# Experts in fixed places of 32-row grains, and a router that picks tile by tile

## What is computed

```python
def _hier_moe(h, w_r1, b_r1, w_r2, b_r2, w13, w2):
    p_grp = softmax(h @ w_r1 + b_r1); grp = argmax(p_grp)              # 4 groups
    p_in = softmax((einsum('nd,gde->nge', h, w_r2) + b_r2)[rows, grp]) # 8 experts in a group
    top_p, top_j = top_k(p_in, 2); top_p /= sum(top_p)
    expert = grp * 8 + top_j;  wts = p_grp[grp] * top_p                # 32 experts in all
    for each expert e, for its tokens:
        g, u = split(h[tok] @ w13[e]); y = (silu(g) * u) @ w2[e]       # 1024 -> 2 x 512 -> 1024
    out[tok] += wts * y
```

## Time and profile before

| | |
|---|---|
| median of 3 runs | 3217.28 us (3216.04 to 3217.42) |
| the profiled execution's own time | 3216.31 us |
| its span, first to last instruction | 3214.7 us |
| PE busy | 2896.9 us (90%) |
| DVE, ACT, POOL busy | 1299.6, 792.7, 689.5 us |
| expert loads L1616, L1857, L1859 | 216 of 2048 KB |
| L1707 (gate_up), L1728 (down) busy | 707.9, 352.8 us |

### The profile page before, as it was taken

The page is one execution under the profiler, slowest core; times in us unless marked ns, Lnnn a source line. Parts: engine busy times, 40 slices in busy tenths (PEclk is TensorE's granted clock), DMA queues, the critical chain, the costliest instruction groups (busy, mean ns, idle before and its releaser), DMA issues. The chain is left out here.

```text
span 3214.7 us, 34383 instructions
## 1 busy us (share of the span) xinstructions
PE 2896.9 (90%) x13041; PEld 1615.1 (50%) x13041; DVE 1299.6 (40%) x2274; ACT 792.7 (25%) x1763; POOL 689.5 (21%) x931
## 2 busy tenths in 40 slices
PE   7999998999999947999999959979999579999993
PEld 3444335888884533444444424468875334443431
DVE  4544204898882252111111154469972521111114
ACT  2211102777771100000000043146641000000001
POOL 2555201555452110010000024510001110000001
PEclk9999999999999958999999979989999789999996
DMA  6334576242413248999999574343322399999995
GB/s 252 100 102 138 199 267 176 52 98 50 99 54 128 92 188 332 412 386 415 383 413 389 216 270 135 88 124 56 67 67 93 130 410 427 426 427 427 426 417 208
DMA packets 205154, 734.36 MB, mean 228 GB/s; under 512 B 29376, under 2 KB 124784, under 8 KB 168896
## 3 DMA queue, kind: packets, MB, share of 16 engines
q1 hardware_dynamic: 104800, 633.33, 52.7%
q10 hardware_dynamic: 84896, 61.07, 5.8%
q0 software_dynamic: 15296, 37.78, 3.0%
HBM read 662.32 MB, written 87.62 MB: 233 GB/s over the span
## 5 line engine op out<-in xcount | busy, mean ns | idle before, releaser
L1707 PE MATMUL psum<-moe_ring,moe_xT 128*64 128x512 f32 (+1 forms) x2240 | 707.9, 602 | 15.6 <-DMA moe_ring<-in_e_w 13.3
L407 PE MATMUL psum<-qkv_w,act_hT 128*128 128x512 f32 x1376 | 612.0, 598 | 1.4 <-ACT act_hT L508 1.3
L1707 PEld LDWEIGHTS psum<-moe_ring,moe_xT 128*64 128x64 f32 (+1 forms) x2240 | 277.3, 162 | 410.4 <-issue 408.4
L407 PEld LDWEIGHTS psum<-qkv_w,act_hT 128*128 128x128 f32 x1376 | 256.6, 192 | 309.2 <-issue 306.9
L1728 PE MATMUL psum<-moe_ring,moe_hT 128*64 128x512 f32 (+1 forms) x1120 | 352.8, 594 | 1.6 <-DVE moe_hT L1808 1.6
L1804 DVE TENSOR_TENSOR moe_hh<-psum,moe_sg 128x512 f32<-128x512 f32 x50 | 34.6, 692 | 668.4 <-PE psum L1707 668.4
L1265 PE MATMUL psum<-wo,out_oT 128*128 128x512 f32 x576 | 255.6, 599 | 1.4 <-DVEq L1281 1.0
L1728 PEld LDWEIGHTS psum<-moe_ring,moe_hT 128*64 128x64 f32 (+1 forms) x1120 | 133.1, 160 | 184.6 <-issue 180.4
L1013 DVE TENSOR_REDUCE att_nmax<-psum 128x1 f32<-128x1280 f32 (+1 forms) x160 | 204.2, 1276 | 29.0 <-PE psum L906 28.0
L906 PE MATMUL psum<-att_kT,att_q 128*128 128x512 f32 (+1 forms) x832 | 198.0, 370 | 10.0 <-ACTq L137 5.1
L969 ACT ACTIVATE att_prob<-psum,att_nmax 128x1280 f32<-128x1280 f32 (+1 forms) x160 | 185.3, 1158 | 56.4 <-DVE att_nmax L1013 53.0
(11 more groups left out here) (252 smaller groups left out, 3301.7 us busy)
## 6 DMA issues: line engine op xcount, KB each, us to landing
moe_ring<-in_e_w SPq DMA_DIRECT2D x216, 2048.0 KB, 16.2
ada_w<-in_ada_w SPq DMA_DIRECT2D x48, 1024.0 KB, 6.5
qk_d<-qkv_stg ACTq DMA_DIRECT2D x112, 256.0 KB, 2.8
att_q<-qk_d SPq DMA_DIRECT2D x32, 640.0 KB, 12.5
att_q<-qk_d SPq DMA_DIRECT2D x64, 256.0 KB, 5.1
qkv_w<-in_a_wqkv SPq DMA_DIRECT2D x6, 2048.0 KB, 9.4
att_kT<-qk_d SPq DMA_DIRECT2D x32, 320.0 KB, 5.7
prep_y<-y_d SPq DMA_DIRECT2D x10, 1024.0 KB, 7.3
```

The lines of the kernel that those rows point to most:

```text
L407: ins = nc.tensor.matmul(psum[:, u.par, :], hT[:, k, u.t * P:(u.t + 1) * P], qw[:, u.C % 2, k], start=(k == 0), stop=(k == KD - 1))
L1707: ins = nc.tensor.matmul(psum[part, bank, :], xT[:, 4 * half + k, part], ring[:, w13[x, half] % RING, k, bank * DE:(bank + 1) * DE], start ...
```

## The change

Experts are ranked by their number of rows at run time, and rank r has a fixed place of `ROOM[l][r]` grains of 32 rows. `STREAM` gives the order of the places by their size; they are laid one behind the other and cut into units of four grains. So a unit can hold parts of one to four experts: 23 units in layer 0 and 19 in layer 1, where there were 27 and 23. Each expert is loaded once in a layer, three pieces: 31 experts in the units, and one of rank `OWN`, with room for 128 rows, which goes through the first round of the fallback loop in place of an overflow block. That makes 192 loads in all, where there were 216. A load waits for the last use of its slot (`FREED`).

In `gate_up` and `down` a unit's parts become calls on 32, 64 or 128 output partitions (`columns`). By `ROOM` and `STREAM` the units are these, in output partitions of the calls:

| calls of a step | layer 0 | layer 1 |
|---|---|---|
| 128 | 7 | 5 |
| 64, 64 | 3 | 2 |
| 64, 32, 32 or 32, 32, 64 | 12 | 6 |
| 32, 32, 32, 32 | 0 | 5 |
| one 64, or 32, 32 (a last half unit) | 1 | 1 |

The picks are made per tile in `post` (`dve_pick`), behind the tile's logits. The placing is rewritten: ranks and tables come from more small matmuls and fewer DVE steps. POOL clears its buffer and issues its small DMA in a part of its own (`pool_route`) ahead of the barrier. The fallback's first product waits for w13 alone.

```diff
-ORDER = [("BBPBBPB" * 4)[1:], ("BP" * 12)[1:]]
-NBIG = [sum(kind == "B" for kind in row) for row in ORDER]
-NSMALL = [2 * sum(kind == "P" for kind in row) for row in ORDER]
-FB0 = [NBIG[l] + NSMALL[l] // 2 for l in range(2)]
+ROOM = [[5] * 3 + [4] * 5 + [3] * 12 + [2] * 11 + [1], [8, 8, 6, 5, 4] + [3] * 5 + [2] * 10 + [1] * 12]
+STREAM = ["4323532243235322432353224323312", "1218121822315213321312263122111"]
+GRAIN = 32
 NFB = 2 * NTOK // P + NE
-NBT = max(FB0) + NFB + 1
-SMALL_AT = 64 * P
+def row_order(l):
+    free = list(range(NE))
+    own = max(r for r in free if ROOM[l][r] == 4)
+    free.remove(own)
+    order = []
+    for digit in STREAM[l]:
+        r = next(r for r in free if ROOM[l][r] == int(digit))
+        free.remove(r)
+        order.append(r)
+    assert not free
+    return order, own
+def row_plan(l):
+    order, own = row_order(l)
+    units, first, at = [], [0] * NE, 0
+    for r in order:
+        first[r] = GRAIN * at
+        for b in range(at, at + ROOM[l][r]):
+            if b // 4 == len(units):
+                units.append([])
+            if not units[-1] or units[-1][-1][0] != r:
+                units[-1].append([r, b % 4, 0])
+            units[-1][-1][2] += 1
+        at += ROOM[l][r]
+    first[own] = P * len(units)
+    return units, first, own
+UNITS, FIRST, OWN = zip(*(row_plan(l) for l in range(2)))
+NU = [len(units) for units in UNITS]
+NBT = max(NU) + 1 + NFB + 1
 EMPTY = 1 << 20
 TILES = [TA, TX]
...
+    def dve_pick(dve, l, t):
+        V_ = nc.vector
+        L = lambda ins: dvec.link(dve, ins)
+        def first_of(val, width, code, top, one):
+            low = lowfirst[:, NE - width:NE]
+            L(V_.reduce_max(top, val, AX))
+            L(V_.scalar_tensor_tensor(code, val, top, low, ALU.is_equal, ALU.mult))
+            L(V_.reduce_max(tops[:, 3:4], code, AX))
+            L(V_.tensor_scalar(one, code, tops[:, 3:4], None, ALU.is_equal))
+        G = logits[:, t, 0:NG]
+        first_of(G, NG, gcode[:, :], tops[:, 0:1], gone[:, :])
+        V_.tensor_scalar(gdist[:, t], G, tops[:, 0:1], None, ALU.subtract)
+        L(V_.tensor_scalar(gone[:, :], gone[:, :], BIG, -BIG, ALU.mult, ALU.add))
+        L(V_.tensor_tensor(egated[:, :].rearrange("p (g e) -> p g e", g=NG), logits[:, t, NG:].rearrange("p (g e) -> p g e", g=NG),
+                           gone[:, :].unsqueeze(2).broadcast_to([P, NG, EPG]), ALU.add))
+        first_of(egated[:, :], NE, ecode[:, :], tops[:, 1:2], chosen[:, 0, t])
+        L(V_.scalar_tensor_tensor(egated[:, :], chosen[:, 0, t], -2 * BIG, egated[:, :], ALU.mult, ALU.add))
+        first_of(egated[:, :], NE, ecode[:, :], tops[:, 2:3], chosen[:, 1, t])
+        V_.tensor_tensor(edist[:, t:t + 1], tops[:, 2:3], tops[:, 1:2], ALU.subtract)
+        L(V_.tensor_tensor(both[:, t], chosen[:, 0, t], chosen[:, 1, t], ALU.add))
+        total = pre[:, t + 1] if t + 1 < TILES[l] else tot[:, :]
+        return V_.tensor_tensor(total, pre[:, t], both[:, t], ALU.add)
...
                 logit(t - 1, 1 - par)
+                dve.wait_ge(s_rld, 2 + T)
+                dvec.link(dve, dve_pick(dve, l, t - 1))
         tile_steps(dve, TILES[l], step, dvec, 2)
         upper(TA * l + TILES[l] - 1, 1)
         logit(TILES[l] - 1, 1)
+        dve.wait_ge(s_rld, 2 + TA * l + TILES[l])
+        dve_pick(dve, l, TILES[l] - 1).then_inc(s_rtp, 1)
 
...
+    def pool_route(pool, l):
+        nc.gpsimd.memset(xg[:, :, :], 0.0).then_inc(s_xz, 1)
+        pool.wait_ge(s_xz, l + 1)
+        if l == 0:
+            pool.dma_start(xg[0:16, 0, 0:P], consts[0:16, 0:P]).then_inc(s_ys[0], 16)
+            pool.wait_ge(s_ys[0], 16)
 
...
+        plan, chunk, ready, done = [], [{}, {}], {}, {}
+        steps, count = [0, 0], 0
         for l in range(2):
-            for i in range(len(UNITS[l]) + 1):
-                w13, w2 = {}, {}
-                if i < len(UNITS[l]):
-                    for half in range(2):
-                        for x in range(len(UNITS[l][i][1])):
-                            w13[x, half] = n
-                            n += 1
-                if i:
-                    for x in range(len(UNITS[l][i - 1][1])):
-                        w2[x] = n
-                        n += 1
-                plan.append((l, i, w13, w2))
-        return plan
-
-    PLAN = chunk_plan()
+            for i in range(NU[l] + 1):
+                new = []
+                parts = {"half0": (i, 0), "up": (i, 1), "down": (i - 1, 2)}
+                for what, (n, piece) in parts.items():
+                    if not 0 <= n < NU[l]:
+                        continue
+                    for r, at, size in UNITS[l][n]:
+                        if (r, piece) not in chunk[l]:
+                            chunk[l][r, piece] = count
+                            new.append((count, r, piece))
+                            count += 1
+                        done[chunk[l][r, piece]] = (l, n, what)
+                    steps[1] += 1
+                    ready[l, n, what] = steps[1]
+                plan.append((l, i, new))
+        return plan, chunk, ready, {n: ready[at] for n, at in done.items()}, count
...
+        for pl, i, new in PLAN:
+            for n, r, piece in new:
+                if pl != l or not first <= n - CHUNKS[0] * l < last:
+                    continue
+                if r not in experts:
+                    experts[r] = sp.value_load(exptab[0:1, r:r + 1], min_val=0, max_val=NE - 1)
+                if n >= RING:
+                    sp.wait_ge(s_used, FREED[n - RING])
+                e = experts[r]
+                src = w2v[:, ds(e, 1), :, :] if piece == 2 else w13v[:, ds(e, 1), 4 * piece:4 * piece + 4, :]
+                sp.dma_start(ring[:, n % RING].rearrange("p k f -> p (k f)"), src.rearrange("p o k f -> p (o k f)")).then_inc(s_ring[n % RING], 16)
...
+        def columns(i):
+            for r, at, size in UNITS[l][i]:
+                while size:
+                    n = max(m for m in (1, 2, 4) if m <= size and at % m == 0)
+                    yield r, slice(GRAIN * at, GRAIN * (at + n))
+                    at, size = at + n, size - n
+        def arrived(i, piece):
+            for r, at, size in UNITS[l][i]:
+                n = CHUNK[l][r, piece]
+                pe.wait_ge(s_ring[n % RING], 16 * (n // RING + 1))
+        def gate_up(i):
             pe.wait_ge(s_xta, xbase + i + 1)
             pe.wait_ge(s_xtd, xbase + i + 1)
-            parts = len(UNITS[l][i][1])
-            rows = P // parts
             for half in range(2):
-                for x in range(parts):
-                    n = w13[x, half]
-                    pe.wait_ge(s_ring[n % RING], 16 * (n // RING + 1))
+                arrived(i, half)
                 for k in range(4):
                     for bank in range(2):
-                        for x in range(parts):
-                            part = slice(x * rows, (x + 1) * rows)
-                            ins = nc.tensor.matmul(psum[part, bank, :], xT[:, 4 * half + k, part], ring[:, w13[x, half] % RING, k, bank * DE:(bank + 1) * DE],
+                        for r, part in columns(i):
+                            ins = nc.tensor.matmul(psum[part, bank, :], xT[:, 4 * half + k, part], ring[:, CHUNK[l][r, half] % RING, k, bank * DE:(bank + 1) * DE],
                                                    start=(half + k == 0), stop=(half == 1 and k == 3))
-                            if k == 3 and bank == 0 and half == 1 and x == parts - 1:
-                                ins.then_inc(s_gate, 1)
-                            if k == 3 and bank == 1:
-                                ins.then_inc(s_used, 1)
-
-        def down(i, w2):
+                        if half == 1 and k == 3 and bank == 0:
+                            ins.then_inc(s_gate, 1)
+                ins.then_inc(s_used, 1)
...
                 for k in range(4):
-                    for x in range(parts):
-                        part = slice(x * rows, (x + 1) * rows)
-                        ins = nc.tensor.matmul(psum[part, 5 + h, :], hT2[:, k, part], ring[:, w2[x] % RING, k, h * HALF:(h + 1) * HALF],
+                    for r, part in columns(i):
+                        ins = nc.tensor.matmul(psum[part, 5 + h, :], hT2[:, k, part], ring[:, CHUNK[l][r, 2] % RING, k, h * HALF:(h + 1) * HALF],
                                                start=(k == 0), stop=(k == 3))
-                        if k == 3 and h == 1:
-                            ins.then_inc(s_used, 1)
-                if h == 0:
-                    ins.then_inc(s_y0, 1)
+                ins.then_inc(s_used if h else s_y0, 1)
 
         def turn_h(i):
...
-            pe.wait_ge(s_ow, 48 * B + 48)
+            pe.wait_ge(s_ow, 32 * B + 32)
...
+            pe.wait_ge(s_ow2, 16 * B + 16)
```

More of the change, by code:

```diff
@@ L1388, in build @@
-    assert A.at <= M.at, (A.at, M.at)
[L1389 to L1399, removed]
+    A = Arena("route1", M_X)
+    placed = A("placed", [P, TA, NE])
+    beyond = A("beyond", [P, TA, NE])
```

(46 more changed lines are left out.)

360 lines of the change are left out of this document (158 added, 202 removed).

## The result

| | before | after |
|---|---|---|
| median of four runs each, side by side | 3216.66 us | 3498.99 us (3496.43 to 3500.75) |
| span of the profiled execution | 3214.7 us | 3494.6 us |
| PE busy | 2896.9 us (90%) | 3206.4 us (92%) |

What follows compares the result with a forecast made beforehand. PE was taken to bound layer 0, DMA layer 1 by a little before the change. Mixed units, fewer units, routing and waits gave +205 in layer 0 and +64 in layer 1: 3216.3 + 205 + 64 + 1 = 3486 us, range 3020 to 3540.

Steps and rivals of the forecast that it cites:

- the likeliest case: Mixed steps drain PE at each change between 64 and 32 columns: 3486 us, own range 3430 to 3540, chance 0.55.
- what was put at nothing: The rest of the kernel, such as one more wait split off in the fallback and the tail: 0 us.
- The mixed step: Expert units with calls on 64 and 32: 1.98 us a step instead of 0.86, 26.9 us more a unit.
- The queueing rival: In mixed units different widths queue but changing is free: 20.6 us more a unit, 3372 us, chance 0.05.
- The gain: Four expert units fewer in each layer, at 22.17 us each: 89 us of PE saved in each.
- The walk: Going through layer 1's units at 4.9 us a load, it found 36 us of waits for weights.
- the +11: Layer 1: 36 us of new waits for weights, against 19 us of old ones and some 6 of slower matmuls.
- Routing: From last logits to first unit: 29 us gained in layer 0 (bounds 15 and 35), 19 in layer 1.
- The overlap rival: In mixed units calls of different sizes run together at no extra price: 3043 us, chance 0.36.
- the dry ring: Layer 1: nine weight slots run empty where units of 32, 32, 32, 32 stand close; +8 us in the overlap case.
- The clock: Rival: PE falls to 1.2 GHz in mixed units, another 41 us each, 4200 us in all; 1 in 100.

Runs made afterwards that it cites:

- e1: The changed kernel with every call of a mixed unit cut to 32 partitions; 3064.80 us, 0.9527 of the kernel before.
- e2: The changed kernel with every call cut to 32 partitions, full units too; 3066.74 us, 0.9529 of the kernel before.
- e3: The changed kernel, mixed sizes kept, but within each half of `gate_up` and `down` all calls of one width first; 3404.09 us, 1.0581 of the kernel before.
- e5: e1 with the picks of all tiles made behind the last logits instead of one by one in `post`; 3128.79 us.
- e4: e1 with POOL's clearing and small DMA put back behind the barrier; 3074.2 us, 0.9553 of the kernel before.
- e7: e1 with most w2 pieces of layer 1 loaded by half, so its experts compute wrongly there; 3034.24 us.

## Why the prediction was right

Predicted 3486 us, measured 3498.99: 13 more, in the likeliest case's own range of 3430 to 3540. Of the 280 us by which the span grew, the terms give 269. Of what was put at nothing, +3.1 us ahead of the logits and -2.6 in the fallback nearly cancel, by luck.

- **The mixed step**, 1.98 us predicted from the neighbours in the earlier trace rows: 1.98 to 1.99 measured. Of its parts, 0.46 for the pairs on 32 stood on no row; the first two pairs of unit 1 start 0.454 us apart. The sum had 12 and 6 units x 26.9: measured (31.80 - 13.92) + (15.95 - 7.03) = 26.8. The change from 64 to 32 acts as the changes of form seen before did, in both directions: the trace agrees with the rule of the Trainium skill (TensorEngine Tiling (Array Packing), Key Properties) that changing the mode drains TensorE. Its other sentence, tiles that run in parallel, holds within one width: 128 MATMULs on 32 columns took 13.94 us in e1 and e2, and 96 of two widths 31.80.
- **The queueing rival** priced the wait of one width for the other at 20.6 a unit and the changes at 6.3. e3 measured 21.4 and 5.4 in one unit. Its size of the first part is right, and as the whole it is wrong, since changing is not free; that widths would queue without the changes stays unshown (see e3).
- **The gain**, four units less in each layer, -89 and -89: it is there. The stretches grew by 238.2 and 89.7, where the mixed units alone give 12 x 26.8 = 322 and 161; the rest is -84 and -71. The second has layer 1's waits for weights in it. The walk's 36 us of waits were 33.6, against 18.9 before; but the +11 took off 6 us for the slow matmuls behind the old waits and put none behind the new ones. Those were 5.5 us before and 8.1 after, so the term is +17, and -71 less 17 is the -89.
- **Routing**: -29.3 of -29, -19.7 of -19, and layer 0's three terms each for itself: from the logits to the counts 4.4 us where it was 13.6 (9 predicted as gain, 9.1 measured), from there to `toktab` 22.7 where it was 34.6 (12 and 11.9), from there to the first gather 1.0 where it was 9.0 (8 and 8.0). e5 gives 4.2 us a tile for the picks, e4 7.6 us for POOL's part.
- **Not predicted**: 3.1 us ahead of the last logits. I had the picks vanish in 6.81 us of DVE's idle time; in the last tile they don't, for 1.9 us.
- **Undervalued, by a little**: each unit of small parts costs 22.3 to 22.6 us between neighbours and not 22.17, and layer 1's waits with what follows them 17 and not 11. By the table the units are 4 us over the forecast in layer 0 and 7 in layer 1, which is the 11 us missing in the span.
- **The overlap rival's 3043**, the case that e1 made: 3064.80, 22 above. Its units were to get 82 us shorter in layer 0 and 52 in layer 1; they got 72.4 and 33.4. In layer 1 stand 59 us of waits for weights, and behind them halves that take 8.4 to 9.4 us instead of 7.07 at a lower granted clock, some 18 us in all, where its bound was DMA's bytes alone and 8 for the dry ring.

The clock did not fall in the mixed units: 1.00 granted in layer 0.

## To carry to other kernels

Packing several small matmuls onto different columns paid here only where all of them, and their neighbours in the queue, had the same width: with the larger ones cut down to the smallest width, 128 MATMULs took what 32 take. One wide call between narrow ones did not merely lose its own share, it made each width run alone. Before a change that saves work by mixing shapes, look in the trace for any place where the shape changes, and measure from the last matmul of one to the first weight load of the next: here that gave 1.98 us for a step that took 1.98 to 1.99.

## What the runs showed of the hardware

- 32 partitions are as fast as 128 when four of them stand side by side: 13.94 us for 128 MATMULs on 32 columns, 13.95 (before) for 64 on 64, 13.90 for 32 on 128. Cutting finer cost 0.5 us a unit, at the joints.
- Neighbouring calls on 64 and on 32 columns did not overlap: a step of both takes 1.98 us, one of a single width 0.86. With each width in a run of its own a `gate_up` takes 28.04 us, what 64 starts 0.43 us apart need.
- A wait has an echo. In e1's layer 1 ten halves (of `gate_up`, or a `down`) behind waits for weights of 2.0 to 7.9 us take 8.4 to 9.4 us instead of 7.07, with 0.75 to 0.84 of the clock granted: some 18 us on top of 59 us of waits. Behind three other waits of 2.0 to 2.5 us a half took 7.07 at 1.00.
- DMA's share alone does not say whether loads are late: with DMA at 0.89 in e7, PE still waited 28.9 us for weights in `gate_up` and 6.8 in the fallback.
